# A hybrid RWKV-7 / attention trunk: the three partial products of each pair tile in one set of 256 columns, brought over by ScalarE alone

## The reference, cut to what matters

```python
h = rms_norm(x, norm_mix_pre[i])
z = h @ w_comb                      # 256 x 2048 by 2048 x (3*1024 + 256 + 3*1024 [+ 32])
y_r, v_r = rwkv7_mix(z_rwkv, ...)
y_a = moba_attention(q, k, v)
y = concatenate([y_r, y_a]) @ w_out[i]
x = x + rms_norm(y, norm_mix_post[i])
m = square(relu(rms_norm(x, ...) @ w_up[i])) @ w_down[i]
x = x + rms_norm(m, norm_mlp_post[i])
```

## Time and profile before

| what | us |
|---|---|
| median of 3 runs | 2481.8 (2481.61 to 2483.28) |
| the profiled execution, its own time | 2484.93 |
| its span, first to last instruction | 2483.0 |
| TensorE busy with matmuls | 2452.8 |
| VectorE busy | 1682.0 |
| ScalarE busy | 1258.4 |
| matmuls on TensorE | 15931 |

### The profile page before, as it was taken

The page is one execution under the profiler, slowest core; times in us unless marked ns, Lnnn a source line. Parts: engine busy times, 40 slices in busy tenths (PEclk is TensorE's granted clock), DMA queues, the critical chain, the costliest instruction groups (busy, mean ns, idle before and its releaser), DMA issues.

```text
span 2483.0 us, 47872 instructions
## 1 busy us (share of the span) xinstructions
PE 2452.8 (99%) x15931; PEld 2062.1 (83%) x15931; DVE 1682.0 (68%) x2809; ACT 1258.4 (51%) x2048; POOL 129.6 (5%) x186
## 2 busy tenths in 40 slices
PE   8999999999999999999999999999999999999998
PEld 7888888788888888888788888887888888888887
DVE  5888887576556566566578888885765565664665
ACT  6555655464444344344456565655553443443443
POOL 3000100000000000000011112100000000000000
PEclk9999999999999999999999999999999999999999
DMA  7444454555656655555554444435556556566554
GB/s 212 140 127 118 133 144 125 190 178 189 194 180 195 194 185 190 192 188 189 163 143 139 121 121 137 136 123 194 180 178 202 187 188 194 179 197 193 183 194 153
DMA packets 437963, 420.06 MB, mean 169 GB/s; under 512 B 19566, under 2 KB 352000, under 8 KB 437888
## 3 DMA queue, kind: packets, MB, share of 16 engines
q1 hardware_dynamic: 434240, 412.55, 53.3%
q0 software_dynamic: 3648, 6.52, 0.9%
HBM read 416.90 MB, written 2.10 MB: 169 GB/s over the span
## 4 chain that ended last, share of the span: by engine, by line
PE 97%; ACT 1%; DVE 1%; DMA 1%; issue 0%; SPq 0%; POOL 0%; DVEq 0%; POOLq 0%; ACTq 0%
PE gemm_bank L538 33%; PE gemm_bank L539 18%; PE gemm_bank L565 11%; PE gemm_bank L567 11%; PE gemm_bank L566 11%; PE gemm_bank L541 2%; PE mix_banks L718 1%; PE mix_banks L725 1%; PE mix_banks L689 1%; PE mix_banks L760 1%; PE mix_banks L765 1%; PE mix_banks L766 1%; PE mix_banks L756 1%; PE mix_banks L590 0%; PE mix_banks L661 0%; PE mix_banks L659 0%
## 5 line engine op out<-in xcount | busy, mean ns | idle before, releaser
L1226 DVE TENSOR_TENSOR b_wlo<-b_raw,b_whi 128x1024 fp32r<-128x1024 f32 x777 | 941.9, 1223 | 532.9 <-ACT b_whi L923 532.0
L538 PE MATMUL gemm_bank<-b_hT,b_whi 128*128 128x512 f32 x3420 | 1247.4, 405 | 1.1 <-DVE b_hT L1278 1.1
L923 ACT ACTIVATE b_whi<-b_raw 128x1024 fp32r<-128x1024 f32 x777 | 812.3, 1057 | 653.4 <-PE gemm_bank L567 413.7
L539 PE MATMUL gemm_bank<-b_hT,b_wlo 128*128 128x256 f32 x3648 | 1012.0, 281 | 0.0
L538 PEld LDWEIGHTS gemm_bank<-b_hT,b_whi 128*128 128x128 f32 x3420 | 643.9, 188 | 150.3 <-issue 2.7
L539 PEld LDWEIGHTS gemm_bank<-b_hT,b_wlo 128*128 128x128 f32 x3648 | 690.3, 189 | 9.8
L565 PE MATMUL gemm_bank<-b_whi,b_mT 128*128 128x512 f32 x1280 | 501.5, 392 | 0.7 <-DVE b_wlo L1226 0.7
L566 PE MATMUL gemm_bank<-b_wlo,b_mT 128*128 128x512 f32 x1280 | 498.4, 389 | 0.0
L567 PE MATMUL gemm_bank<-b_whi,b_mT 128*128 128x512 f32 x1280 | 498.3, 389 | 0.0
L565 PEld LDWEIGHTS gemm_bank<-b_whi,b_mT 128*128 128x128 f32 x1280 | 240.3, 188 | 50.5 <-ACT b_whi L923 1.5
L567 PEld LDWEIGHTS gemm_bank<-b_whi,b_mT 128*128 128x128 f32 x1280 | 240.3, 188 | 50.1
(11 more groups left out here) (234 smaller groups left out, 1741.3 us busy)
## 6 DMA issues: line engine op xcount, KB each, us to landing
b_raw<-in_w_up SPq DMA_DIRECT2D x256, 512.0 KB
b_raw<-in_w_down SPq DMA_DIRECT2D x256, 512.0 KB
b_raw<-in_w_in SPq DMA_DIRECT2D x384, 256.0 KB
b_raw<-in_w_out SPq DMA_DIRECT2D x60, 512.0 KB
b_raw<-in_w_in SPq DMA_DIRECT2D x8, 512.0 KB
b_xt<-in_x SPq DMA_DIRECT2D x8, 256.0 KB, 5.2
b_raw<-in_w_out SPq DMA_DIRECT2D x8, 256.0 KB
out<-b_xt SPq DMA_DIRECT2D x8, 256.0 KB, 2.4
```

What stands on the lines that cost most here:

```text
L538: mm(bank[b0 + b][:, :], whi[r][:, cols], pair, start=first, stop=False)
L539: m = mm(bank[b0 + b][:, 0:SEQ], wlo[r][:, cols], act[:, kt, 0, :], start=False, stop=False)
L923: f(whi[r][:, :], raw[r][:, :, :].rearrange("p a b -> p (a b)"), ACT.Copy).then_inc(hi_done, 1)
L1226: tt(wlo[r][:, :], flat(raw[r][:, :, :]), whi[r][:, :].bitcast(F32), ALU.subtract).then_inc(lo_done, 1)
```

## The change

In the pairs alone, `tick` is called with `wide=False`. It then makes three products of 256 columns for each tile and `kt`: `whi` by hi, `whi` by lo, `wlo` by hi, all into the left 256 columns of the bank. ScalarE copies the finished tile from there straight into `zt` (`whole`), and gives `tile_out` itself; `xl`, `half_out` and VectorE's add are no longer used there. The waits on `half_out` of other stages are lowered by 48 per layer, since 48 tiles of a layer no longer count.

```diff
-            def tick(k, d, j, act, kt, b0, first, last, free=(None, None)):
+            def tick(k, d, j, act, kt, b0, first, last, free=(None, None), wide=True):
...
                     if free[b] is not None:
                         pe.wait_ge(tile_out, free[b])
+                    if not wide:
+                        to = bank[b0 + b][:, 0:SEQ]
+                        mm(to, whi[r][:, cols], act[:, kt, 0, :], start=first, stop=False)
+                        mm(to, whi[r][:, cols], act[:, kt, 1, :], start=False, stop=False)
+                        m = mm(to, wlo[r][:, cols], act[:, kt, 0, :], start=False, stop=last)
+                        if last and b == 0:
+                            m.then_inc(first_sum, 2)
+                        continue
                     if not last:
                         mm(bank[b0 + b][:, :], whi[r][:, cols], pair, start=first, stop=False)
...
-                group(k, 0, l and t - 1, hT, 0)
+                group(k, 0, l and t - 1, hT, 0, {}, False)
...
-                group(k + 4, 0, t, hT, 2, {8: first_key_norms})
+                group(k + 4, 0, t, hT, 2, {8: first_key_norms}, False)
...
+            def whole(k, d, tiles, b0, j):
+
+                act.wait_ge(first_sum, tiles + 2)
+                f(zt[:, j, 1:], bank[b0][:, 0:SEQ], ACT.Copy).then_inc(tile_out, 1)
+                act.wait_ge(slot_used, k + 4 * d + 1)
+                f(zt[:, j + 1, 1:], bank[b0 + 1][:, 0:SEQ], ACT.Copy).then_inc(tile_out, 1)
...
                     def finish(g):
-                        halves(k + 11 + 4 * g, i * 3, t + 4 + 2 * g + i * 6, (2, 2, 0)[g + 1])
+                        whole(k + 11 + 4 * g, i * 3, t + 4 + 2 * g + i * 6, (2, 2, 0)[g + 1], (2, 4, 0)[g + 1])
...
-            def sums(tiles, b0, dest, n=2):
+            def sums(tiles, b0, dest, without, n=2):
                 for b in range(n):
-                    dve.wait_ge(half_out, tiles + b + 1)
+                    dve.wait_ge(half_out, tiles + b + 1 - without)
                     tt(dest(b), bank[b0 + b][:, 0:SEQ], xl[:, b, :], ALU.add).then_inc(tile_out, 1)
...
-                finish(-1)
                 key_inverse(n)
...
-                    if lv == 1:
-                        finish(0)
...
-                    if c == 1:
-                        finish(1)
```

More of the change, by code:

```diff
@@ L545, in tick, with group @@
                     m.then_inc(slot_used, 1)
-            def group(k, d, tiles, act, b0, after={}):
+            def group(k, d, tiles, act, b0, after={}, wide=True):
                 free = (None, None) if isinstance(tiles, int) and tiles <= 0 else (tiles - 1, tiles)
@@ L552, in group @@
                     tick(k + kt // SK, d, kt % SK, act, kt, b0, kt == 0, kt == KT - 1,
-                         (None, None) if kt else free)
+                         (None, None) if kt else free, wide)
                     if kt in after:
@@ L623, in pair_ticks @@
                     tick(k + x // SK, d, x % SK, hT, kt, (2, 0, 2)[g], kt == 0, kt == KT - 1,
-                         (None, None) if kt else (out - 1, out))
+                         (None, None) if kt else (out - 1, out), False)
             def last_ticks(a, b, k, tiles):
@@ L1132, in _ @@
                 k, t = start[l, "pairs"]
-                group(k, 0, t, 0)
+                for j in range(4):
+                    hi(k + LEAD + j)
+                whole(k + 3, 0, t, 0, 0)
                 hi(k + 4 + LEAD)
@@ L1147, in finish @@
                     if g < 1:
-                        halves(k + 95 + 4 * g, 0, t + 46 + 2 * g, 2)
+                        whole(k + 95 + 4 * g, 0, t + 46 + 2 * g, 2, 2 * g + 4)
                 mixer(l, PAIRS - 1, PAIRS * l + PAIRS - 1, t + 46,
@@ L1349, in key_square, with mixer @@
                     ALU.mult).then_inc(e["kk_sq"], 1)
-            def mixer(l, i, n, tiles, step, finish, more=True):
+            def mixer(l, i, n, tiles, step, more=True):
                 V = n + 1
@@ L1590, in _ @@
                 splits(k, 0, 2)
-                sums(t, 2 * (1 - l), lambda b: zt[:, 3 + b, 1:])
+                sums(t, 2 * (1 - l), lambda b: zt[:, 3 + b, 1:], 48 * l)
                 if l:
@@ L1594, in _ @@
                     lo(k + LEAD)
-                    sums(t, 2, lambda b: zt[:, 5, 1:], 1)
+                    sums(t, 2, lambda b: zt[:, 5, 1:], 48 * l, 1)
                 if l == 0:
@@ L1610, in _ @@
                 k, t = start[l, "pairs"]
-                def place(g):
-                    return lambda b: zt[:, 2 * g + b, 1:]
                 splits(k, 0)
-                sums(t, 0, place(0))
                 lo(k + 4 + LEAD)
@@ L1622, in turn @@
                 def turn(i):
-                    def finish(g):
-                        sums(t + 4 + 2 * g + i * 6, (2, 2, 0)[g + 1], place((1, 2, 0)[g + 1]))
                     def step(j):
                         lo(k + 8 + j + LEAD, i * 3)
-                    mixer(l, i, PAIRS * l + i, t + 4 + i * 6, step, finish)
+                    mixer(l, i, PAIRS * l + i, t + 4 + i * 6, step)
                 lo(k + 6 + LEAD)
                 loop(dve, PAIRS - 1, turn)
-                def finish(g):
-                    if g < 1:
-                        sums(t + 46 + 2 * g, 2, place(g + 2))
                 def step(j):
@@ L1639, in step @@
                         lo(k + 92 + j + LEAD)
-                mixer(l, PAIRS - 1, PAIRS * l + PAIRS - 1, t + 46, step, finish, False)
+                mixer(l, PAIRS - 1, PAIRS * l + PAIRS - 1, t + 46, step, False)
                 k, t = start[l, "out"]
@@ L1673, in up_turn @@
                                 for b in range(2):
-                                    dve.wait_ge(half_out, T + b + 1)
+                                    dve.wait_ge(half_out, T + b + 1 - 48 * (l + 1))
                                     tt(hid(b), bank[2 * g + b][:, 0:SEQ], xl[:, b, :], ALU.add).then_inc(up_sum, 1)
```

## The result

The changed kernel takes 2493.05 us (median of 6 runs, 2491.73 to 2493.89) against 2482.3 us (6 runs, 2481.61 to 2485.07) of the kernel before: ratio 1.004, interval 1.003 to 1.005. It is slower by 10.75 us. The forecast said 2502, in a range of 2486 to 2517, and slower; the sign holds and the time lies in the range, and the change is half as large as was forecast.

The account below looks back on a forecast made before the run. The prediction took TensorE's own list of matmuls to bound the kernel. It added 1536 splits at 13.6 ns, +20.9 us, to the median 2481.8 us, with nothing for other engines, and said 2502 us, range 2486 to 2517.

Parts of the forecast that it names:

- TensorE sets the time, and the other engines' work is hidden: Whole kernel: TensorE, busy 99% of the span, runs through its own list while VectorE and ScalarE keep ahead.
- 1536 splits, each on the path: Pairs: 1536 wide products become 3072 narrow ones, adding 1536 matmuls and weight loads, all on TensorE's path.
- A narrow product costs 120.0 ns, with its own load, in the same columns or not: Pairs: each 256-column product takes 120.0 ns including its load; nothing charged for adding up in the same columns.
- 13.6 ns a split, in each of 96 steps a turn: Pairs: each tile and step goes from 346.4 to 360.0 ns, +13.6 ns x 1536 = +20.9 us.
- the ends of the fills: Switches between fills and small matmuls: cost unchanged, since a group begins and ends with a load as before; nothing charged.
- the split costs nothing: Rival, pairs: a narrow product costs half a wide one, so the time stays at 2482 us; chance 0.12.
- an upper bound of the new cost (+53 us): Pairs: the MLP's 353.3 ns, surplus charged to the narrow product, makes it 126.9 ns; +34.3 ns a step, +53 us.
- The narrow one costs 346.4 - 226.4: Pairs: the alternating period less the wide-after-wide distance gives 120.0 ns for a narrow product.
- Gains on other engines bring nothing: VectorE loses 96 adds, 40 us of 1682, hidden behind TensorE; ScalarE's copies stay the same in number: no gain.
- The rival of waits that don't show: Changes from fills to mixer matmuls: hidden waits, at most 51 us, absorb added time; faster, down to 2464 us; chance 0.05.
- The rival of the loads: Pairs: narrow products wait for their loads, 122.4 to 126.9 ns each; +32 to +53 us, 2514 to 2535; chance 0.18.
- the free split: Pairs: two narrow products cost no more than one wide; three narrow take 346 ns, time stays at 2482 us; chance 0.12.

Follow-up runs that it names:

- the third experiment: The kernel before, with wide products split into narrow ones in the MLP's first product instead of the pairs, old hand-over kept: 2493.83 against 2481.65 us, ratio 1.0049.

## Why the prediction was right, and where it was off

- *TensorE sets the time, and the other engines' work is hidden*: right. Of VectorE's 38 us less, 2.7 reach the turns, and that by one position in its list.
- *1536 splits, each on the path*: right, 17467 matmuls. *A narrow product costs 120.0 ns, with its own load, in the same columns or not*: right inside every fill that was looked at; beside the mixer's products and in a fill's first steps the distances differ (113 to 125 ns).
- *13.6 ns a split, in each of 96 steps a turn*: this is the term that was too large, on the side of what is removed. The measured average is 8.2 ns. The forecast took 346.4 ns from one long fill and charged it to every step. Two things are wrong with that. The smaller one is the pace: fills at 353 ns were there too, and only inside a fill at the fast pace does the split cost 13.3 to 13.6 ns; the long fills cost 10.8 a split, 2.0 us less in all than forecast. The larger one is the ends of the fills, of which the prediction said "nothing": nearly half of a turn's steps lie in fills of two or four, and there a split cost 2.4 and 7.0 ns, 5.1 us less in all. In a fill of two the rival "the split costs nothing" was nearly true.
- The slower pace had been read, in the MLP, but was charged to the narrow product and so made an upper bound of the new cost (+53 us); as a price of what the change removes it would have made a lower one: 360.0 - 353.3 = 6.7 ns, x 1536 = +10 us. For the MLP the third experiment bears this out (7.0). That it comes near the 10.75 us of the change is luck: most fills of the pairs didn't go at that pace.
- *The narrow one costs 346.4 - 226.4*: the difference meets 120.0 by chance. In the earlier trace rows the wide one takes 0.23 us to its narrow neighbour and that one some 0.115 to the next wide one (232 and 115 ns by the starts over the fill). The price of a step was read as a whole and isn't touched by this.
- *Gains on other engines bring nothing*: off by 2.7 us in the fourteen turns, to the same side as the term above. The rival of waits that don't show had the mechanism, and it was held unlikely since waits on another engine should vary from turn to turn. This one doesn't: the lists of all engines repeat exactly, and so does a wait between them.
- *The rival of the loads* (122 to 127 ns a narrow product) fell with 120.0 in a row of nothing but narrow ones; *the free split* fell with 360 against 346 to 353. The estimate by the 2.5 ns of the Trainium skill, "TensorE: Matmul & The Clock Gate", section "Back-to-back issue gap", was 2485.6 us; the run is 7.5 us above it, so the rule gives a third of the change. (The page gives it for a matmul by itself, without a budget for the load that each one has here.)
- Sum over the fourteen turns: 11.0 us for the products less 2.7 for the wait, 8.3, against 8.08 in the windows. The other 2.7 us of the 10.75 can't be placed: the remaining 192 splits lie outside the windows, but in the two traces the time outside is the same (1785.4 us before, 1785.2 after). The profiled execution of the kernel before took 2484.93 us, 2.6 more than its median, and that is the difference.

## What to carry to other kernels

When a change replaces a stream of matmuls, price the removed form in several stretches of the trace, by distances of starts over a dozen periods, and not only the new one: here the new form was known to the nanosecond and the old one to 2%, which is as much as the whole effect. And count how many of the steps lie in short fills between other work: a price from the middle of a long fill held for half of the steps at best, and in fills of two it was nearly nothing. A wait that repeats exactly, and is shorter than the part of a matmul's row that overlaps the next, is found only by comparing the same step at different iterations (0.24 us after line 760 of the third chunk, 0.14 elsewhere). Where two shapes of matmul alternate, try another order of the same products: two and two gave 0.36% here for one edit.

## What the runs showed that was not expected

- The same alternation of a 512-column and a 256-column product goes at 346.4 or at 353.3 ns a step, stretch by stretch: the fast pace is the usual one in the pairs, the slow one in the MLP. Of 138 fills of eight or more steps in the kernel before, 135 kept their pace to the end, and the other three show a longer gap in the middle. A row of nothing but narrow ones has one pace, 120.0.
- Next to the mixer's small products the split costs less than inside a fill, down to 2.4 ns in fills of two steps. What pays for the rest is open.
- Wide, wide, narrow, narrow makes the kernel 8.3 us shorter, nearly all outside the pairs, and with four wide, four narrow in the MLP 3.9 of it are left. What in the order decides is open: the number of passages between the shapes doesn't explain it by itself, and no run took the phase in which a fill begins by itself.
- Moving 0.4 to 0.8 us of work within VectorE's list, which is idle for a sixth of a turn, freed one wait of 0.19 us and made another of 0.19 to 0.37 us in the same chain.
